# Four transformer layers on one core: the first two weight jobs behind a norm or a merge run as one, row by row

## The chip, the cores and the metric

The kernel runs on one core of one Trainium2 chip. The time is device microseconds (us) for one execution. The profiled execution is a separate one, with its own time.

## The reference, cut to what matters

The input is x, 256 tokens by 1024 features in float32. Two blocks of two layers each are applied one after the other; the kernel calls them A and B.

```python
# block A, each of 2 layers
h = rms_norm(x) @ w_in                      # three kinds of attention, their outputs in mix
x = x + mix @ w_o
gate, up = split(rms_norm(x) @ w_gate_up)   # 2816 + 2816 columns
x = x + (silu(gate) * up) @ w_down
# block B, each of 2 layers
u = rmsnorm(x) @ w_in                       # pooling, convolution, dilated attention, three gates
merged = g0 * br_a + g1 * br_b + g2 * br_c
x = x + rmsnorm(merged @ w_out)
x = x + rmsnorm(memory_cross_attention(rmsnorm(x), mem))
u = rmsnorm(x) @ w_up                       # ua, ub: 2816 + 2816 columns
x = x + rmsnorm((silu(conv(ua)) * ub) @ w_down)
```

## The kernel before, in words

**Layout.** x lies with features on the partitions: 8 row tiles of 128 features by 256 tokens (KD = 8, T = 256). A float32 product is made of three matmuls on rounded halves: high and low part of the weights (`weights_hi`, `weights_lo`) and of x (`x_hi`, `x_lo`), without low times low. One 128x128 weight tile with its three matmuls of 256 columns is the unit of all dense work.

**Jobs and chunks.** The dense work is a list of jobs (`q0`, `gate3`, `out1`, ...). Most make two output tiles of 128 features, so they read 16 weight tiles, first the 8 rows of the first output tile, then those of the second. The weights are packed on the host in the order of use into chunks of at most 12 tiles (128x1536). SyncE loads chunks into 5 raw buffers. ScalarE makes `weights_hi` from a chunk (`split_hi`, L636), VectorE makes `weights_lo` (`split_lo`, L647); chunks 0 and 1 of each layer are done by GpSimd instead (`pool_lo`, L660, chosen by `of_pool`). There are 4 split buffers: chunk c may be split when TensorE has released chunk c-4. `cut()` begins a new chunk early.

**Order.** The lists `order_a` and `order_b` are written by hand, and every engine walks the same list and does its part of each entry, strictly in that order. At each job entry ScalarE and VectorE first split all chunks up to `last_chunk(job) + 2`, and then do the job's own work. `last_chunk(name)` is the chunk of the last row of the last tile, `tiles[-1][-1][1]` (L622). An engine that waits at one entry does nothing of the later ones.

```python
# order_a around gate0, order_b around the merge and out0
("job", "o2"), ("front", ("n2", 1)), ("front", ("n2", 2)), ("job", "gate0"), ("adds", "n2"),
("job", "up0"), ("mean", "n2"), ("job", "gate1"), ("factor", "n2")
("job", "ma3"), ("merge_hi", 2), ("merge_lo", 2), ("job", "mb3"), ("job", "mc3"), ("merge_hi", 3),
("merge_lo", 3), ("job", "out0"), ("mem_split", 0), ("job", "out1"), ("mem_split", 1), ("job", "out2"),
("root_table", "out"), ("job", "out3"), ("job", "mk0a"), ("mem_keys", "mk0a"), ("norm", "p1"), ("spread", "p1")
```

**Behind a norm.** `front` entries write x_hi (ScalarE, L890) and x_lo (VectorE, L900) row tile by row tile, as x becomes known. The factor of the norm is applied later; `squares`, `adds`, `mean` and `factor` find it beside the products: ScalarE squares x (L894), GpSimd adds the pairs (L834, L836), VectorE adds the rest (L855, L858), TensorE sums over the partitions (L908), ScalarE takes the root (L914). In block B the norms p1, p2 and p3 of an output are a serial chain between two jobs: ScalarE squares and scales what out3, mo3 or down3 made (`scalar_y`, L2123 and L2125), adds, TensorE L867, ScalarE L817, VectorE, TensorE L877, then VectorE renews x by row tiles (L2338, L2340). Meanwhile TensorE runs a few `keep_busy` matmuls on zeros (L708).

**The first job** behind a norm or the merge runs in `first_products`: first all products with x_hi (L732, L735), then those with x_lo (L741). Its partner, the second job, runs in the ordinary loop `products` (L775, L777, L778). The pairs are gate0 and up0 in A, q0 and k0, out0 and out1, ua0 and ub0 in B. q0, out0 and ua0 take the high products by row (`ROWS_FIRST`); gate0 takes them tile by tile.

**The merge.** For each of four column pairs i, the jobs ma, mb, mc give the branches; VectorE multiplies each by its gate (L2430) and adds (L2434), ScalarE writes x_hi (L2225), VectorE x_lo (L2357). out0 to out3 follow.

**PSUM.** A job takes the bank used least recently, of 3 banks, or of 6 if its name is in a list; `start_use` waits until the bank's last reader is done.

## Time and profile before

| what | us |
|---|---|
| median of 3 runs | 1700.1 |
| lowest, highest of them | 1691.17, 1700.37 |
| the profiled execution, its own time | 1694.4 |
| its span, first to last instruction | 1692.6 |
| TensorE busy in the span | 1653.9 |
| VectorE, ScalarE, GpSimd busy | 1194.5, 895.7, 114.7 |

A matmul counts as busy until its modelled end, and matmuls overlap, so the pace of TensorE is read from the distance between starts. In a timeline row the first number is the start in us from the span's start, the second how long the row lasts; x4 at the end means four instructions merged.

### The profile page before, as it was taken

To read this page: it belongs to the slowest core of one execution; us is meant where nothing else is said; L and a number is where in the kernel's file an instruction comes from. 1 tells how busy PE (TensorE), PEld (TensorE's weight loads), DVE (VectorE), ACT (ScalarE), POOL (GpSimd) and SP (SyncE) were. 2 spreads that over 40 slices of the span, in tenths; PEclk is the share of its full clock that TensorE was granted. 3 is DMA by queue.
4 is the path that set the end of the run, shared out by engine and by line. 5 is a ranking of instruction groups with operands and counts; after the bars stand their busy time and mean duration, and the time that the engine had idled before them with its cause. 6 is when DMAs were issued, how large, how long until landed. Compare 5 with 4: busy or idle time off the path is not lost.

```text
span 1692.6 us, 31850 instructions
## 1 busy us (share of the span) xinstructions
PE 1653.9 (98%) x13590; PEld 1591.9 (94%) x13590; DVE 1194.5 (71%) x1745; ACT 895.7 (53%) x1366; POOL 114.7 (7%) x72
## 2 busy tenths in 40 slices
PE   9989999999999999999999999999999999999997
PEld 9978999999879999989999989999899999899997
DVE  5887767547976775476858758983667768669963
ACT  5575544454675444544545765554435446655542
POOL 2020000020110000210000110000200001010000
PEclk9999999999999999999999999999999999999999
DMA  8313555553225655555345435654445345345650
GB/s 291 110 58 119 198 188 181 177 189 129 94 76 187 207 198 181 202 185 182 118 149 170 155 109 196 209 182 168 165 167 169 132 160 195 119 138 197 207 188 37
DMA packets 52830, 274.31 MB, mean 162 GB/s; under 512 B 6096, under 2 KB 6736, under 8 KB 52560
## 3 DMA queue, kind: packets, MB, share of 16 engines
q1 hardware_dynamic: 52544, 271.22, 46.9%
q8 instruction: 107, 1.75, 0.4%
q10 hardware_dynamic: 144, 1.05, 0.2%
q14 instruction: 35, 0.29, 0.1%
HBM read 271.19 MB, written 1.05 MB: 161 GB/s over the span
## 4 chain that ended last, share of the span: by engine, by line
PE 77%; DVE 15%; ACT 4%; issue 2%; DMA 1%; POOL 0%; SPq 0%; ACTq 0%; DVEq 0%; POOLq 0%
PE bank L775 16%; PE bank L777 16%; PE bank L778 16%; DVE weights_lo L647 3%; PE scores L775 3%; PE scores L777 3%; PE scores L778 3%; PE heads L775 2%; PE heads L777 2%; PE heads L778 2%; ACT weights_hi L636 1%; PE scores L1849 1%; ACT probs L1170 1%; PE heads L1877 1%; DVE x_lo L900 1%
## 5 line engine op out<-in xcount | busy, mean ns | idle before, releaser
L647 DVE TENSOR_TENSOR weights_lo<-raw,weights_hi 128x1536 fp32r<-128x1536 f32 (+2 forms) x344 | 584.1, 1715 | 232.3 <-ACT weights_hi L636 232.0
L636 ACT ACTIVATE weights_hi<-raw 128x1536 fp32r<-128x1536 f32 (+4 forms) x352 | 499.8, 1440 | 191.1 <-PE bank L778 82.3
L775 PE MATMUL bank<-x_hi,weights_lo 128*128 128x256 f32 (+1 forms) x1600 | 450.1, 281 | 1.0 <-DVE weights_lo L647 1.0
L777 PE MATMUL bank<-x_lo,weights_hi 128*128 128x256 f32 (+1 forms) x1600 | 443.5, 277 | 0.0
L778 PE MATMUL bank<-x_hi,weights_hi 128*128 128x256 f32 (+1 forms) x1600 | 443.4, 277 | 0.0
L775 PEld LDWEIGHTS bank<-x_hi,weights_lo 128*128 128x128 f32 (+1 forms) x1600 | 298.9, 187 | 6.8 <-issue 4.1
L777 PEld LDWEIGHTS bank<-x_lo,weights_hi 128*128 128x128 f32 (+1 forms) x1600 | 300.0, 187 | 2.0 <-issue 2.0
L778 PEld LDWEIGHTS bank<-x_hi,weights_hi 128*128 128x128 f32 (+1 forms) x1600 | 298.7, 187 | 0.0
L775 PE MATMUL bank<-hidden_hi,weights_lo 128*128 128x256 f32 x704 | 196.3, 279 | 0.7 <-DVE hidden_lo L2194 0.7
L777 PE MATMUL bank<-hidden_lo,weights_hi 128*128 128x256 f32 x704 | 196.0, 278 | 0.0
L778 PE MATMUL bank<-hidden_hi,weights_hi 128*128 128x256 f32 x704 | 196.0, 278 | 0.0
L775 PEld LDWEIGHTS bank<-hidden_hi,weights_lo 128*128 128x128 f32 x704 | 132.8, 189 | 1.2 <-DVE hidden_lo L2194 1.1
L777 PEld LDWEIGHTS bank<-hidden_lo,weights_hi 128*128 128x128 f32 x704 | 132.9, 189 | 0.0
L778 PEld LDWEIGHTS bank<-hidden_hi,weights_hi 128*128 128x128 f32 x704 | 132.1, 188 | 0.0
L775 PE MATMUL scores<-x_hi,weights_lo 128*128 128x256 f32 x416 | 115.5, 278 | 0.9 <-DVE weights_lo L647 0.9
L777 PE MATMUL scores<-x_lo,weights_hi 128*128 128x256 f32 x416 | 115.4, 277 | 0.0
L778 PE MATMUL scores<-x_hi,weights_hi 128*128 128x256 f32 x416 | 115.4, 277 | 0.0
L834 POOL TENSOR_TENSOR squares<-squares 128x512 f32<-128x512 f32 x28 | 52.3, 1868 | 829.6 <-ACT squares L2123 638.1
L775 PEld LDWEIGHTS scores<-x_hi,weights_lo 128*128 128x128 f32 x416 | 78.1, 188 | 1.2 <-issue 1.2
L777 PEld LDWEIGHTS scores<-x_lo,weights_hi 128*128 128x128 f32 x416 | 78.5, 189 | 0.0
L778 PEld LDWEIGHTS scores<-x_hi,weights_hi 128*128 128x128 f32 x416 | 78.2, 188 | 0.0
L775 PE MATMUL heads<-x_hi,weights_lo 128*128 128x256 f32 x256 | 71.5, 279 | 0.4 <-DVE weights_lo L647 0.4
(410 smaller groups left out, 3392.3 us busy)
## 6 DMA issues: line engine op xcount, KB each, us to landing
raw<-in_w_b SPq DMA_DIRECT2D x194, 768.0 KB, 4.2
raw<-in_w_a SPq DMA_DIRECT2D x120, 768.0 KB, 4.2
raw<-in_w_a SPq DMA_DIRECT2D x16, 512.0 KB, 3.7
raw<-in_w_b SPq DMA_DIRECT2D x10, 512.0 KB, 3.9
raw<-in_w_b SPq DMA_DIRECT2D x2, 752.0 KB, 4.6
raw<-in_w_a SPq DMA_DIRECT2D x2, 736.0 KB, 7.7
raw<-in_w_b SPq DMA_DIRECT2D x2, 720.0 KB, 4.9
raw<-in_w_a SPq DMA_DIRECT2D x2, 672.0 KB, 6.7
```

The source lines that it names most:

```text
L636: nc.scalar.activation(whi[c % SPLIT][:, 0:n], raw[c % RAW][:, 0:n], ACT.Copy).then_inc(*s.mark("weights_hi", c))
L647: nc.vector.tensor_tensor(wlo[c % SPLIT][:, 0:n], raw[c % RAW][:, 0:n], whi[c % SPLIT][:, 0:n].bitcast(F32), ALU.subtract).then_inc(*s.mar ...
L775: ins = nc.tensor.matmul(dst, wl, xh, start=start, stop=False, skip_group_check=skip)
L777: nc.tensor.matmul(dst, wh, xl, start=False, stop=False, skip_group_check=skip)
L778: ins = nc.tensor.matmul(dst, wh, xh, start=False, stop=stop, skip_group_check=skip)
L834: nc.gpsimd.tensor_tensor(sq[:, 0:2, :], sq[:, 0:2, :], sq[:, 2 * n:2 * n + 2, :], ALU.add).then_inc(*s.mark("sq_pairs", (tag, n)))
L900: nc.vector.scalar_tensor_tensor(out=XL[:, k, :], in0=X[:, k, :], scalar=gains(k), in1=XH[:, k, :].bitcast(F32), op0=ALU.mult, op1=ALU.sub ...
L1170: ins = nc.scalar.activation(PA[c][:, m, :], score_bank[c][:, m * T:(m + 1) * T], ACT.Exp, scale=f[:, m:m + 1], bias=ROW[:, r + m:r + m + ...
L1849: ins = nc.tensor.matmul(dil_scores(h, m, g), QKB[r, f // 2, m * P:(m + 1) * P], QKB[r, 6 + f // 2, 0:dil_tiles(m) * P], start=True, stop= ...
L1877: ins = nc.tensor.matmul(out_bank[rows, m * P:(m + 1) * P], VB[:, kt, f * DHD:(f + 1) * DHD], PTB[:, g * kts + kt, :], start=(n == 0), sto ...
```

## The change: what it does

1. The four pairs of jobs (`PAIRED`) run as one in `first_products`: per row tile k the high products of all four output tiles, row by row, and after all rows the low products in the same order. Both banks are taken at the start. gate0 and up0 go through the rows in the order 6, 7, 0 to 5 (`ROW_ORDER`).
2. Their weights are packed in that order (`Both`): a row has 4 tiles, a chunk 3 rows, so a pair takes chunks of 12, 12 and 8 tiles. With the cuts, gate0/up0 has chunks 26 to 28 of A, q0/k0 0 to 2, out0/out1 43 to 45 and ua0/ub0 59 to 61 of B. Before, gate0 had 26 and 27 with 8 tiles each, up0 28 and 29; both streams keep 72 and 104 chunks. down3 of both blocks begins a chunk.
3. The splits move: at the end of the layer before, chunk 2 of B too (`scalar_next_chunks`, `vector_next_chunks`); `AHEAD` says how far each job splits; out0's chunks with rows 3 to 7 (44, 45) get their low part on GpSimd; gate0 splits up to `last_chunk + 1`, and the front of row tiles 4 and 5 up to `last_chunk("gate0")`. At `squares` only n2 still splits first.
4. `adds` of n3 stands before ua0. down2 in A and p3_sum in B take the second oldest bank; out0 and out1 may use all 6.

```diff
                 stream.cut()
+class Both:
+    def __init__(self, names, stream, source, operand, cols, row_order):
+        self.names = names
+        self.jobs = [Job(name, stream, source, operand, [], []) for name in names]
+        for job, c in zip(self.jobs, cols):
+            job.tiles = [[None] * KD for _ in c]
+        for k in row_order:
+            for job, c in zip(self.jobs, cols):
+                for t, columns in enumerate(c):
+                    job.tiles[t][k] = (k,) + stream.add(source, k * P, P, columns)
+PAIRED = (("gate0", "up0"), ("q0", "k0"), ("out0", "out1"), ("ua0", "ub0"))
+ROW_ORDER = {"gate0": (6, 7, 0, 1, 2, 3, 4, 5)}
+def rows_of(name):
+    return ROW_ORDER.get(name, tuple(range(KD)))
...
+
+    def both(first, second, source, operand, *c):
+        pair = Both((first, second), stream, source, operand, c, rows_of(first))
+        jobs.update(zip(pair.names, pair.jobs))
...
     stream.cut()
-    for i in range(KF // 2):
-        job(f"gate{i}", "w_gate_up", "x2", cols(i * T, 2), full, cut=i == 0)
+    both("gate0", "up0", "w_gate_up", "x2", cols(0, 2), cols(FF, 2))
+    stream.cut()
+    for i in range(1, KF // 2):
+        job(f"gate{i}", "w_gate_up", "x2", cols(i * T, 2), full)
         job(f"up{i}", "w_gate_up", "x2", cols(FF + i * T, 2), full)
     for i in range(4):
         job(f"down{i}", "w_down", "h", cols(i * T, 2), even(KF))
-        if i < 2:
+        if i < 3:
...
     q, k, v, gates = 4 * CW, 4 * CW + AW, 4 * CW + 2 * AW, 4 * CW + 3 * AW
-    for i in range(AW // T):
-        job(f"q{i}", "w_in_2", "x", cols(q + i * T, 2), full, cut=i == 0)
+    both("q0", "k0", "w_in_2", "x", cols(q, 2), cols(k, 2))
+    stream.cut()
+    for i in range(1, AW // T):
+        job(f"q{i}", "w_in_2", "x", cols(q + i * T, 2), full)
...
         job(f"mc{i}", "w_branch_c_2", "dil", cols(i * T, 2), even(2))
-    for i in range(4):
+    stream.cut()
+    both("out0", "out1", "w_out_2", "merged", cols(0, 2), cols(T, 2))
+    for i in range(2, 4):
...
         job(f"mo{i}", "w_mo_2", "memo", cols(i * T, 2), even(MEM_H))
-    for i in range(KF2 // 2):
-        job(f"ua{i}", "w_up_2", "x3", cols(i * T, 2), full, cut=i == 0)
+    stream.cut()
+    both("ua0", "ub0", "w_up_2", "x3", cols(0, 2), cols(FF2, 2))
+    for i in range(1, KF2 // 2):
+        job(f"ua{i}", "w_up_2", "x3", cols(i * T, 2), full)
         job(f"ub{i}", "w_up_2", "x3", cols(FF2 + i * T, 2), full)
     for i in range(4):
+        if i == 3:
+            stream.cut()
...
-            def __init__(self, number, s, stream, jobs, uses, operands, wide_ring):
+            def __init__(self, number, s, stream, jobs, uses, operands, wide_ring, second_oldest=()):
                 self.number, self.s, self.stream, self.jobs = number, s, stream, jobs
                 self.names, self.freed, self.at = [name for name, _ in uses], dict(uses), {}
                 oldest = list(range(BANKS + 3))
                 for name in self.names:
-                    n = next(n for n in oldest if n < BANKS or name.startswith(wide_ring))
+                    n = [n for n in oldest if n < BANKS or name.startswith(wide_ring)][1 if name in second_oldest else 0]
...
                 self.of_pool = set()
-                self.hi_ahead, self.pool_ahead = 0, 0
+                self.hi_ahead, self.lo_ahead, self.pool_ahead = 0, 0, 0
...
                 after.hi_next, after.s.layer, after.s.writing = 0, m, "scalar"
-                split_hi(after, act, m, 1)
+                upto = 1 if after is plan_a else 2
+                split_hi(after, act, m, upto)
                 pl.hi_next, pl.s.layer = here, layer
-                after.hi_ahead = 2
+                after.hi_ahead = upto + 1
+        def vector_next_chunks(pl, dve, l):
+            after, m = next_layer(pl, l)
+            if after is plan_b:
+                here, layer = pl.lo_next, pl.s.layer
+                after.lo_next, after.s.layer, after.s.writing = 2, m, "vector"
+                split_lo(after, dve, m, 2)
+                pl.lo_next, pl.s.layer = here, layer
+                after.lo_ahead = 3
...
         WAITS = {"p1_sum": 3, "p1_factor": 3, "p2_sum": 7, "p2_factor": 3, "ua0": 7, "p3_sum": 7, "p3_factor": 3, "q0": 7}
-        def first_products(pl, pe, l, name, hi_ready):
-            s, job = pl.s, pl.jobs[name]
-            ps = start_use(pl, pe, l, name)
-            keep_busy(ps, WAITS.get(name, 0) if name != "q0" or l else 0)
-            if name == "cq0" and l == 0:
+        def first_products(pl, pe, l, names, hi_ready):
+            s, jobs = pl.s, [pl.jobs[name] for name in names]
+            banks = [start_use(pl, pe, l, name) for name in names]
+            keep_busy(banks[0], WAITS.get(names[0], 0) if names[0] != "q0" or l else 0)
+            if names[0] == "cq0" and l == 0:
                 pe.wait_ge(*O.at(0, "eps"))
-                keep_busy(ps, 44)
-            hi, lo, ready = pl.operands[job.operand]
-            steps = [(t, k) + job.tiles[t][k][1:] for t in range(len(job.tiles)) for k in range(KD)]
-            by_rows = sorted(steps, key=lambda step: step[1]) if name in ROWS_FIRST else steps
+                keep_busy(banks[0], 44)
+            hi, lo, ready = pl.operands[jobs[0].operand]
+            steps = [(j, t, k) + job.tiles[t][k][1:] for j, job in enumerate(jobs) for t in range(len(job.tiles)) for k in range(KD)]
+            by_rows = sorted(steps, key=lambda step: rows_of(names[0]).index(step[2]))
+            paired, last_row = len(jobs) > 1, rows_of(names[0])[-1]
             for low in (False, True):
-                for n, (t, k, c, o, rows, width) in enumerate(steps if low else by_rows):
-                    dst = ps[0:width, t * T:(t + 1) * T]
+                for j, t, k, c, o, rows, width in by_rows if paired or (not low and names[0] in ROWS_FIRST) else steps:
+                    dst = banks[j][0:width, t * T:(t + 1) * T]
+                    whole = low and k == last_row and t == len(jobs[j].tiles) - 1
                     if not low:
                         if c != pl.chunk_at:
                             pe.wait_ge(*s.at(l, *pl.raw_mark(c)))
                             pl.chunk_at = c
-                        if t == 0:
+                        if j + t == 0:
                             pe.wait_ge(*s.at(l, *hi_ready(k)))
-                        ins = nc.tensor.matmul(dst, wlo[c % SPLIT][0:rows, o:o + width], hi[0:rows, k, :], start=(n == 0), stop=False,
+                        first = t == 0 and k == rows_of(names[0])[0]
+                        ins = nc.tensor.matmul(dst, wlo[c % SPLIT][0:rows, o:o + width], hi[0:rows, k, :], start=first, stop=False,
                                                skip_group_check=True)
                         free_split(pl, ins)
                         nc.tensor.matmul(dst, whi[c % SPLIT][0:rows, o:o + width], hi[0:rows, k, :], start=False, stop=False,
                                          skip_group_check=True)
                     else:
-                        if t == 0:
+                        if j + t == 0:
                             pe.wait_ge(*s.at(l, *ready(k)))
-                            pl.ready.add((job.operand, k))
-                        ins = nc.tensor.matmul(dst, whi[c % SPLIT][0:rows, o:o + width], lo[0:rows, k, :], start=False, stop=(k == KD - 1),
+                            pl.ready.add((jobs[0].operand, k))
+                        ins = nc.tensor.matmul(dst, whi[c % SPLIT][0:rows, o:o + width], lo[0:rows, k, :], start=False, stop=(k == last_row),
                                                skip_group_check=True)
-                        if n < len(steps) - 1:
+                        if not whole:
                             free_split(pl, ins)
                         if o + width == pl.stream.used[c]:
                             pl.unfreed = c
-            ins.then_inc(*s.mark("filled", name))
+                        if whole:
+                            ins.then_inc(*s.mark("filled", names[j]))
...
             "mix": (MH, ML, lambda k: ("dif_lo", k // 2) if k < DIF_H else ("mix_lo", k)),
-            "h": (HH, HL, lambda k: ("hidden_lo", k))}, ("gate", "up", "o3", "dq0", "dk0", "g0", "g1", "kv", "flip_dq", "flip_dk0", "flip_g"))
+            "h": (HH, HL, lambda k: ("hidden_lo", k))}, ("gate", "up", "o3", "dq0", "dk0", "g0", "g1", "kv", "flip_dq", "flip_dk0", "flip_g"), ("down2",))
...
                     nc.tensor.matmul(ps[:, 0:2], ones[0:DIF_D, :], ROW[0:DIF_D, 40:42], start=True, stop=True).then_inc(*s.mark("filled", "lam_sum"))
-                elif kind == "job" and name in ("cq0", "gate0"):
-                    first_products(pl, pe, l, name, lambda k: ("norm_hi", ("n1" if name == "cq0" else "n2", k)))
+                elif kind == "job" and name == "cq0":
+                    first_products(pl, pe, l, ("cq0",), lambda k: ("norm_hi", ("n1", k)))
+                elif kind == "job" and name == "gate0":
+                    first_products(pl, pe, l, ("gate0", "up0"), lambda k: ("norm_hi", ("n2", k)))
+                elif kind == "job" and name == "up0":
+                    continue
...
                     scalar_front(pl, act, l, tag, i, lambda k: gain_a(g, k), lambda k: ("x_new", f"{source}{k // 2}"))
+                    if (tag, i) == ("n2", 2):
+                        split_hi(pl, act, l, pl.last_chunk("gate0"))
...
                     if name not in NO_SPLITS:
-                        split_hi(pl, act, l, pl.last_chunk(name) + 2)
+                        split_hi(pl, act, l, pl.last_chunk(name) + (1 if name == "gate0" else 2))
...
                     tag, i = name
+                    if (tag, i) == ("n2", 2):
+                        split_lo(pl, dve, l, pl.last_chunk("gate0"))
...
                     if name not in NO_SPLITS:
-                        split_lo(pl, dve, l, pl.last_chunk(name) + 2)
+                        split_lo(pl, dve, l, pl.last_chunk(name) + (1 if name == "gate0" else 2))
                     ps = pl.bank(name)
                     if name in ("dv0", "dv1"):
                         continue
                     elif name[0] == "o" or name.startswith("down"):
                         i = int(name[-1])
+                        if name == "down3":
+                            vector_next_chunks(pl, dve, l)
...
         order_b += [("front", ("n3", i)) for i in range(4)] + [("squares", "n3"),
-                    ("job", "ua0"), ("adds", "n3"), ("job", "ub0"), ("mean", "n3"), ("job", "ua1"), ("factor", "n3")]
+                    ("adds", "n3"), ("job", "ua0"), ("job", "ub0"), ("mean", "n3"), ("job", "ua1"), ("factor", "n3")]
...
             "merged": (XH, XL, lambda k: ("merged_lo", k // 2)), "memo": (OMH, OML, lambda k: ("memo_lo", k)),
-            "h": (HH2, HL2, lambda k: ("hidden_lo", k))}, ("ua", "ub", "ma", "mb", "mc"))
-        plan_b.of_pool = {0, 1}
+            "h": (HH2, HL2, lambda k: ("hidden_lo", k))}, ("ua", "ub", "ma", "mb", "mc", "out0", "out1"), ("p3_sum",))
+        merge_chunks = {jobs_b["out0"].tiles[0][k][1] for k in range(3, KD)}
+        plan_b.of_pool = {0, 1} | merge_chunks
+        AHEAD = {"mc3": 3, "out0": 1, "out2": 3, "out3": 3, "mo2": 3, "mo3": 3, "q0": 1, "ua0": 1}
...
                 elif kind == "job" and name in first_of_b:
-                    first_products(pl, pe, l, name, first_of_b[name])
+                    names = next((pair for pair in PAIRED if pair[0] == name), (name,))
+                    first_products(pl, pe, l, names, first_of_b[name])
+                elif kind == "job" and name in ("k0", "out1", "ub0"):
+                    continue
...
                 elif kind == "squares":
-                    split_hi(pl, act, l, pl.last_chunk({"n1": "q0", "n2": "mq0", "n3": "ua0"}[name]) + 2)
+                    if name == "n2":
+                        split_hi(pl, act, l, pl.last_chunk("mq0") + 2)
...
                     if name not in own_splits:
-                        split_hi(pl, act, l, pl.last_chunk(name) + (3 if name in ("out1", "out2", "out3") else 2))
+                        split_hi(pl, act, l, pl.last_chunk(name) + AHEAD.get(name, 2))
...
             pl, s = plan_b, B
-            pl.lo_next = 0
+            pl.lo_next, pl.lo_ahead = pl.lo_ahead, 0
...
                     if name not in own_splits:
-                        split_lo(pl, dve, l, pl.last_chunk(name) + (3 if name in ("out1", "out2", "out3") else 2))
+                        split_lo(pl, dve, l, pl.last_chunk(name) + AHEAD.get(name, 2))
+                    if name == "down3":
+                        vector_next_chunks(pl, dve, l)
...
                 elif kind == "job":
-                    pool_lo(pl, pool, l, pl.last_chunk(name) + 2)
+                    pool_lo(pl, pool, l, pl.last_chunk(name) + (3 if name == "mc3" else 2))
```

## Rows read from the trace of the kernel before

**Rows 1.** Who waited for whom, TensorE: us in total, times, longest

```profile
PE scores L732 <- ACT x_hi L890: 2.5, 6, 0.6
```

**Rows 2.** Timeline of TensorE, first and last of 39 matmuls on end

```profile
799.75 0.28 PE L775 MATMUL bank<-x_hi,weights_lo 128*128 128x256 f32 x1
...
804.06 0.28 PE L778 MATMUL bank<-x_hi,weights_hi 128*128 128x256 f32 x1
```

**Rows 3.** Timeline of TensorE in A, layer 0: first of gate0, first of gate1

```profile
173.65 0.28 PE L732 MATMUL scores<-x_hi,weights_lo 128*128 128x256 f32 x1
...
187.10 0.36 PE L775 MATMUL bank<-x_hi,weights_lo 128*128 128x256 f32 x1
```

**Rows 4.** Timelines of VectorE, GpSimd and ScalarE beside gate0 and up0

```profile
174.97 4.23 DVE L900 SCALAR_TENSOR_TENSOR x_lo<-x,gains_a,x_hi 128x256 fp32r<-128x256 f32 x4
...
179.12 3.41 DVE L647 TENSOR_TENSOR weights_lo<-raw,weights_hi 128x1536 fp32r<-128x1536 f32 x2
...
178.11 0.81 POOL L836 TENSOR_TENSOR squares<-squares 128x256 f32<-128x256 f32 x1
...
187.28 0.26 ACT L914 ACTIVATE norm_root<-turned,row 128x4 f32<-128x4 f32 x1 [4.33 <-PE turned L908]
```

**Rows 5.** GpSimd's split L660: count and durations in ns, min/median/max

```profile
L660 POOL TENSOR_TENSOR weights_lo<-raw,weights_hi x8: 2351/2400/2612, 9.7 to 1183.6; 128x1024 fp32r<-128x1024 f32 x8
```

**Rows 6.** Timelines from the merge to p1 in B, layer 0, by engine

```profile
914.19 0.63 ACT L2225 ACTIVATE x_hi<-t 128x512 fp32r<-128x512 f32 x1 [4.04 <-DVE t L2434]
...
916.60 0.39 PE L732 MATMUL bank<-x_hi,weights_lo 128*128 128x256 f32 x1 [0.25 <-DVE t L2430]
...
923.75 0.60 ACT L2123 ACTIVATE squares<-bank 128x512 f32<-128x512 f32 x1 [0.41 <-PE bank L741]
...
924.96 1.71 ACT L1981 ACTIVATE mem_hi<-mem,gains_b 128x256 fp32r<-128x256 f32 x4
...
928.99 0.28 PE L775 MATMUL bank<-x_hi,weights_lo 128*128 128x256 f32 x1
...
935.98 1.28 ACT L812 ACT_TABLE_LOAD   x1
...
937.38 2.88 ACT L636 ACTIVATE weights_hi<-raw 128x1536 fp32r<-128x1536 f32 x2
...
940.17 0.58 ACT L2123 ACTIVATE squares<-bank 128x512 f32<-128x512 f32 x1
...
942.68 0.42 DVE L858 TENSOR_TENSOR squares<-squares 128x256 f32<-128x256 f32 x1
```

**Rows 7.** Timelines of ScalarE and TensorE at the passage from A to B

```profile
701.22 1.28 ACT L2650 ACT_TABLE_LOAD   x1
...
704.66 2.49 ACT L890 ACTIVATE x_hi<-x,gains_b 128x256 fp32r<-128x256 f32 x6
...
706.52 0.36 PE L732 MATMUL bank<-x_hi,weights_lo 128*128 128x256 f32 x1 [0.82 <-DVE x L1673]
```

**Rows 8.** Timelines of ScalarE, TensorE and VectorE at ua0, B, layer 0

```profile
994.00 1.07 ACT L636 ACTIVATE weights_hi<-raw 128x1024 fp32r<-128x1024 f32 x1
...
1003.50 0.36 PE L732 MATMUL scores<-x_hi,weights_lo 128*128 128x256 f32 x1
...
1007.49 3.25 DVE L900 SCALAR_TENSOR_TENSOR x_lo<-x,gains_b,x_hi 128x256 fp32r<-128x256 f32 x8
...
1018.46 0.36 PE L775 MATMUL heads<-x_hi,weights_lo 128*128 128x256 f32 x1
```

**Rows 9.** Timelines of GpSimd and TensorE at q0, B, layer 1

```profile
1188.74 0.73 POOL L836 TENSOR_TENSOR squares<-squares 128x256 f32<-128x256 f32 x1
...
1194.32 0.36 PE L732 MATMUL bank<-x_hi,weights_lo 128*128 128x256 f32 x1
...
1209.61 0.36 PE L775 MATMUL bank<-x_hi,weights_lo 128*128 128x256 f32 x1
```

**Rows 10.** Busy time by engine, granted clock, DMA share and GB/s, one stretch

```profile
143.50:150.00 6.50, 4.72 (x27) 4.75 (x28) 5.61 (x9) 2.30 (x9) 0.00 (x0) 0.74 0.49 147
```

3 lines of the change are left out of this document (added).

## The prediction

> **What bounds the kernel now.** I read the page first: TensorE is busy for 1653.9 of 1692.6 us, so only the places where it waits, and what the edits put in its way, can move the time. The waits of TensorE come next: the largest entry that the change aims at is the wait of the high products for x_hi, 2.5 us in six pieces [rows 1]. Short waits fall under that view's threshold, so I took the pace from the timeline: 38 steps from 799.75 to 804.06, 0.1134 us a matmul [rows 2]. A pair of jobs is 96 matmuls, 10.9 us at this pace. Whatever lies between the first matmul of a pair and the first of the next job beyond 10.9, and 0.4 for the four small `mean` matmuls, is lost. gate0 and up0 take 13.45 [rows 3]: 2.2 lost. ua0 and ub0 take 14.96 [rows 8]: 3.7 lost. q0 and k0 of B's second layer take 15.29 [rows 9]: 4.0. out0 and out1 take 12.39 and start 0.4 late [rows 6]: 1.9. q0 of B's first layer, and cq0 of A's second, wait 0.8 each for a bank [rows 7]. With both layers that is 4.4 + 7.4 + 4.0 + 3.8 + 1.6 = 21 us, 1.25%: the most that the change can win.
>
> **The change part by part.** Two prices first. ScalarE: two high splits of 1536 columns run from 937.38 to 940.17, so 1.4 each [rows 6]; 1024 columns take 1.1 [rows 8]. VectorE: two low splits take 3.41, so 1.7 each [rows 4]; two thirds of it for 1024, 1.2.
>
> *ua0 and ub0.* The first high product starts when row 0 of x_hi is there, at 1003.50. Rows then come about every 0.65 us: VectorE has renewed x when it turns to x_lo at 1007.5 [rows 8], and the last x_hi follows 1.0 later. A row now feeds 8 matmuls, 0.91 us, so TensorE waits 0.3 in all, ends the high products at 1011.05 and the low ones at 1014.7; with the mean ua1 starts at 1015.1 and not 1018.46 [rows 8]: 3.4 won. Against it: chunks 60 and 61 are both split at mo2. ScalarE had one of 1024 at 994.00 [rows 8]; now 1.4 + 1.1, so the squares of mo2 come 0.75 later, and VectorE has 1.7 + 1.2 of low splits where GpSimd adds squares. They block each other (below), and the sum of p2 is 1.3 late, on the serial chain. Net 2.1 won, 4.2 in two layers; bounds 2 and 7.
>
> *out0 and out1, low parts on GpSimd.* GpSimd took 2.40 us for 1024 columns [rows 5]; in proportion 3.6 for 1536, less some fixed part 3.5. ScalarE splits chunk 44 at job mb3, and `merge_hi 2` stands before that: x_hi of the third pair starts at 914.19 [rows 6], so chunk 44's high part is ready at 916.2 and chunk 45's at 917.7. GpSimd is through with 44 at 920.4 and with 45 at 924.6. TensorE starts at 916.2 (the bank wait is gone, 0.4 won), wants chunk 44 for row 3 at 918.9 and chunk 45 at 923.3: it waits 1.6 and 1.3. The low products end at 930.15; out2 started at 928.99 before [rows 6], so 1.2 is lost here.
>
> How GpSimd and VectorE hinder each other is in the timeline: eight x_lo take 3.25 us alone [rows 8], four take 4.23 while GpSimd adds squares [rows 4]. [...]
>
> *out0 and out1, the work behind them.* This is the larger part. Both jobs now end together at 930.0, and ScalarE walks its list: y of out0 1.2 (from 923.75 to 924.96), four mem_hi 1.6, chunk 47, y of out1, four mem_hi, chunks 48 and 49, y of out2, the root table 1.4 (935.98 to 937.38), chunks 50 and 51, and only then the squares of out3 [rows 6]. Before, out0's y and chunk 47 were done by 928. Sum: 3 x 1.2 + 2 x 1.6 + 5 x 1.4 + 1.4 = 15.2, so the squares start at 945.3, not 940.17 [rows 6]. VectorE's low part of chunk 51 and the adds behind it end at 948.1, not 943.1 [rows 6]. Nothing covers it: TensorE has mk0a, and then the serial chain of p1. It is 5.0 later with the 1.2 of before in it; 10.0 in two layers. Bounds 3 (if ScalarE catches up) and 12.
>
> *gate0 and up0.* The x_hi rows cost nothing any more: rows 6 and 7 were there first, a row lasts 0.91. But the order of rows meets `last_chunk`: it takes the chunk of row 7, and by `ROW_ORDER` row 7 is in the first of three chunks, 26, not 28. So the new split at the front asks for 26 and does nothing, gate0 asks for 27, up0 for 28. Chunk 28 comes after `adds`, which waits for GpSimd (its last add ends at 178.92, [rows 4], now 0.5 later since chunk 27 has 1536 columns) and for the x_lo that it held up: ready at 182.2. TensorE wants it for row 4 at 173.65 + 48 x 0.1134 = 179.1. It waits 3.2; rows 4 and 5 to 184.1, the low products to 187.75, the mean to 188.2. Before, up0 asked for chunk 31; now chunk 29 is asked for at gate1, and on ScalarE `mean` stands before gate1: L914 waits for TensorE's mean (187.28 after 187.1 before, [rows 4]). So root 0.2, high split 1.4, low split 1.7: chunk 29 is ready at 191.7. gate1 starts at 191.8, not 187.10 [rows 3]: 4.7 lost, 9.4 in two layers. Bounds: 2.2 won a layer if both splits were in time, 5.5 lost.
>
> *q0 and k0, first layer of B.* ScalarE now waits for chunk 2's buffer until 2.7 us (8 tiles) before down3's end, 0.8 and some before 706.52, so 702.8, then 1.1, to 703.9. Behind it stand the sine tables and the root table, 3.45 from 701.22 to 704.66, which ended just in time [rows 7]. x_hi starts at 707.35 and TensorE at 708.0, not 706.52 [rows 7]: 1.5 later, of which 0.1 comes back. 1.4 lost; bounds -0.8 and 2.5. cq0 in A's second layer loses the 0.8 wait and waits 0.1 for x_hi: 0.7 won.
>
> *q0 and k0, second layer of B.* The rows bring 3.1 as at ua0. But GpSimd has chunks 0 and 1 with 1536 columns: 3.5 each and not 2.4 [rows 5], and VectorE chunk 2 at the same moment. GpSimd's last add for p3 ended at 1189.47 [rows 9], 0.8 before it was wanted; now all of them end at 1191 to 1192.5, and the chain of p3 is 1.9 late. The rest of the win goes into the mean, whose sum is ready at 1209.2. q1 starts at 1209.7 against 1209.61 [rows 9]: 0, bounds -3 and 2.
>
> *The rest.* 16 tiles more or less in a chunk and the other cuts change no totals: the same tiles, 72 and 104 chunks, DMAs of the same bytes. down2's and p3_sum's banks have been free for 15 us.
>
> **Sum.** 9.4 + 10.0 + 1.4 - 0.7 + 0 - 4.2 = +15.9 us on the profiled execution's 1694.4: 1710.3. That execution was 5.7 under the median; the four times shown have the mean 1696.5, which gives 1712.4. I say 1712, 0.7% over the median. About 1%, 17 us, is what a measurement of this kernel tells from no change, since its own runs lie 9 us apart.
>
> **The rivals.** *The rows win.* All splits hide, and 15 to 21 us of the lost time go: 1676 to 1682. It needs chunks 28 and 29 early, against the code's own order, and ScalarE free behind out1. Chance 0.04. *One of the two large costs is absent* (chunk 29 in time, or the squares of out3 in time): 1700 to 1704. For it speaks that ScalarE is busy only 53% of the span; against it that it works its list in order. 0.26. *Forecast*: 1706 to 1717, 0.45. *The clock falls, and the time ends slower:* TensorE would idle 3.3 to 4 us at four new places, chunks 28 and 29 in both layers of A and before p1's sum in B. [...] Four to six such stretches add 7 to 10: 1719 to 1722. 0.25, with other late waits of the same kind in it.
>
> **How the numbers follow.** Slower by over 1% (over 1717) has the last rival and a part of the forecast's upper end: 0.36. Faster by over 1% (under 1683) is the first: 0.03. The rest, 0.61, is within 1%. The range goes from 1696, under the half-cost case, to 1723, the clock's.
>
> **What would show it.** In the profile after: TensorE waiting for weights_lo (L647) before row 4 in gate0 and again at gate1, 3 us each, in both layers, with ScalarE's root directly before chunk 29; L660 with 12 entries, four of them in the merges, 3.5 us long; the squares of out3 5 us later after the merge; ua1 2 us earlier. If gate1 starts within 12 us of gate0, my reading of `last_chunk` is wrong, and the time is near 1703; if the squares of out3 follow out3 at once, the same. If both, the kernel is faster than before.

## The result, and the profile after

The changed kernel takes 1725.97 us (median of 4: 1718.01 to 1728.56), the kernel before 1698.69 beside it (median of 4: 1691.17 to 1700.37). The ratio is 1.0163, 95% interval 1.0139 to 1.0188: 1.6% slower. The profiled execution took 1724.51, its span is 1722.7, 30.1 more than before. (The medians differ by 27.3: the profiled execution of before lay 4.3 under its median.) From the page of the changed kernel, busy time, share and instructions:

```profile
PE 1659.4 (96%) x13590; PEld 1600.9 (93%) x13590; DVE 1205.8 (70%) x1741; ACT 894.3 (52%) x1366; POOL 135.6 (8%) x76
```

TensorE's busy time rose by 5.5 us only (1653.9 before), so most of the 30 is idle time. GpSimd has 20.9 us more (114.7 before), its larger and added splits.

**Waits.** TensorE's waits in the changed kernel (us in total, times, longest), against [rows 1]:

```profile
PE bank L834 <- DVE weights_lo L691: 11.5, 6, 3.6
PE bank L926 <- DVE squares L917: 10.8, 5, 2.8
PE scores L790 <- POOL weights_lo L704: 4.8, 4, 1.5
PE scores L790 <- DVE weights_lo L691: 4.6, 2, 2.5
PE bank L790 <- ACT x_hi L949: 2.4, 1, 2.4
PE bank L834 <- DVE gates L2486: 1.2, 2, 0.6
```

The six waits of the high products for x_hi [rows 1] are gone; the one of 2.4 is another, new one, at q0 of B's first layer. In their place TensorE waits for low parts of weights: from VectorE in gate0 (4.6) and at gate1 (3.6 in each layer, 7.2 of the 11.5), from GpSimd in out0 (4.8), and for the squares ahead of a norm's sum (L926; 2.65 at p1 of B's first layer).

**gate0, up0 and gate1** in A's first layer, timelines of ScalarE, VectorE and TensorE, against [rows 3, 4]:

```profile
178.33 1.05 ACT L680 ACTIVATE weights_hi<-raw 128x1024 fp32r<-128x1024 f32 x1
189.18 0.26 ACT L973 ACTIVATE norm_root<-turned,row 128x4 f32<-128x4 f32 x1 [9.81 <-PE turned L967]
189.34 2.84 ACT L680 ACTIVATE weights_hi<-raw 128x1536 fp32r<-128x1536 f32 x2
...
176.88 4.22 DVE L959 SCALAR_TENSOR_TENSOR x_lo<-x,gains_a,x_hi 128x256 fp32r<-128x256 f32 x4
181.02 0.41 DVE L914 TENSOR_TENSOR squares<-squares 128x256 f32<-128x256 f32 x1
181.81 1.22 DVE L691 TENSOR_TENSOR weights_lo<-raw,weights_hi 128x1024 fp32r<-128x1024 f32 x1
190.85 1.76 DVE L691 TENSOR_TENSOR weights_lo<-raw,weights_hi 128x1536 fp32r<-128x1536 f32 x1 [1.19 <-ACT weights_hi L680]
...
183.08 0.39 PE L790 MATMUL scores<-x_hi,weights_lo 128*128 128x256 f32 x1 [2.46 <-DVE weights_lo L691]
192.75 0.55 PE L834 MATMUL bank<-x_hi,weights_lo 128*128 128x256 f32 x1 [3.61 <-DVE weights_lo L691]
```

gate0 starts at 175.02. Chunk 28 is the one of 1024 columns: its high part is done at 179.38, its low part stands behind four x_lo and the adds (181.81) and ends at 183.03; TensorE goes on at 183.08. Chunk 29's high part stands behind the root of the norm (189.18), its low part ends at 192.61, and gate1 starts at 192.75: 17.73 behind gate0, not 13.45 [rows 3]. The second layer has 17.60 against 13.11.

**The clock.** Three stretches: start and end, length, busy time and number of instructions by engine (TensorE first), granted clock, DMA share and GB/s:

```profile
186.00:189.00 3.00, 3.00 (x29) 3.00 (x27) 0.00 (x0) 0.00 (x0) 0.00 (x0) 1.00 0.12 51
192.00:198.50 6.50, 5.75 (x27) 5.78 (x28) 5.61 (x4) 4.21 (x4) 0.00 (x0) 0.50 0.75 238
724.50:727.50 3.00, 3.00 (x16) 3.00 (x15) 2.34 (x6) 3.00 (x8) 0.09 (x1) 0.50 1.00 392
```

Behind the 3.6 us wait at gate1 the granted clock is 0.50, matmuls start 213 ns apart instead of 113, and the stretch loses 2.8 us; the second layer 1.6 (0.50 from 544.0 to 546.5), and q0 of B, behind its 2.4 us wait, 1.6. With fillers in the wait at gate1 (run 2 below) the clock behind it is 1.00, and 4.2 us of this come back.

**out0, out1 and the work behind them** in B's first layer, timelines of GpSimd, VectorE, ScalarE and TensorE, against [rows 5, 6]:

```profile
935.94 7.83 POOL L704 TENSOR_TENSOR weights_lo<-raw,weights_hi 128x1536 fp32r<-128x1536 f32 x2 [177.96 <-ACT weights_hi L680]
...
935.84 0.69 DVE L2511 TENSOR_TENSOR t<-t,merge_part 128x512 f32<-128x512 f32 x1
936.57 0.69 DVE L2507 SCALAR_TENSOR_TENSOR merge_part<-gates,bank 128x512 f32<-128x512 f32 x1
937.29 3.13 DVE L2511 TENSOR_TENSOR t<-t,merge_part 128x512 f32<-128x512 f32 x1
941.19 3.13 DVE L2432 SCALAR_TENSOR_TENSOR x_lo<-t,x_hi 128x512 fp32r<-128x512 f32 x1 [0.77 <-ACT x_hi L2300]
...
949.54 0.60 ACT L2197 ACTIVATE squares<-scores 128x512 f32<-128x512 f32 x1 [7.08 <-PE scores L799]
964.77 0.58 ACT L2197 ACTIVATE squares<-bank 128x512 f32<-128x512 f32 x1
...
939.92 0.39 PE L790 MATMUL scores<-x_hi,weights_lo 128*128 128x256 f32 x1 [1.51 <-POOL weights_lo L704]
943.82 0.38 PE L790 MATMUL scores<-x_hi,weights_lo 128*128 128x256 f32 x1 [0.90 <-POOL weights_lo L704]
967.80 0.61 PE L926 MATMUL bank<-const,squares 128*128 128x2 f32 x4 [2.65 <-DVE squares L917]
```

GpSimd's two splits take 3.9 each, and TensorE waits 1.51 and 0.90 for them. ScalarE stands idle for 7.1 us and then has the work of both jobs at once: the squares of out3 begin at 964.77, 29.2 behind out0's start (935.53); before it was 23.6 [rows 6]. Two instructions of VectorE that take 0.69 take 3.13 beside GpSimd's splits; both have two inputs in SBUF. L2507, with an input from PSUM, took 0.69 in between. The slow two end at 940.42 and 944.32, each 0.55 behind the end of the split that was running (939.86 and 943.77).

### The profile page after: what moved, and what is told of

Its sections match the earlier page's. It is cut to its first block, busy times and chain, and to the rows that moved or that the text cites. A ratio compares the mean times of both kernels' runs of the same rounds, so it can differ in the third digit from the quotient of the medians.

```text
span 1722.7 us, 31845 instructions
## 1 busy us (share of the span) xinstructions
PE 1659.4 (96%) x13590; PEld 1600.9 (93%) x13590; DVE 1205.8 (70%) x1741; ACT 894.3 (52%) x1366; POOL 135.6 (8%) x76
## 4 chain that ended last, share of the span: by engine, by line
PE 75%; DVE 13%; ACT 6%; issue 3%; POOL 2%; DMA 0%; SPq 0%; ACTq 0%; DVEq 0%; POOLq 0%
PE bank L834 15%; PE bank L837 14%; PE bank L836 14%; PE scores L834 3%; PE scores L837 3%; PE scores L836 3%; DVE weights_lo L691 3%; ACT weights_hi L680 3%; PE heads L837 1%; PE heads L836 1%; PE heads L834 1%; POOL weights_lo L704 1%; DVE x_lo L959 1%; ACT probs L1229 1%; PE heads L1948 1%
## 5 line engine op out<-in xcount | busy, mean ns | idle before, releaser
L834 PE MATMUL bank<-x_hi,weights_lo 128*128 128x256 f32 (+1 forms) x1536 | 436.3, 284 | 9.9 <-DVE weights_lo L691 8.7
L836 PE MATMUL bank<-x_lo,weights_hi 128*128 128x256 f32 (+1 forms) x1536 | 429.2, 279 | 0.0
L837 PE MATMUL bank<-x_hi,weights_hi 128*128 128x256 f32 (+1 forms) x1536 | 429.2, 279 | 0.0
L834 PEld LDWEIGHTS bank<-x_hi,weights_lo 128*128 128x128 f32 (+1 forms) x1536 | 289.0, 188 | 16.2 <-issue 12.8
L836 PEld LDWEIGHTS bank<-x_lo,weights_hi 128*128 128x128 f32 (+1 forms) x1536 | 291.3, 190 | 2.0 <-issue 2.0
L837 PEld LDWEIGHTS bank<-x_hi,weights_hi 128*128 128x128 f32 (+1 forms) x1536 | 288.7, 188 | 0.0
L704 POOL TENSOR_TENSOR weights_lo<-raw,weights_hi 128x1536 fp32r<-128x1536 f32 (+1 forms) x12 | 39.3, 3287 | 922.6 <-ACT weights_hi L680 922.6
```

What stands on the lines that cost most here:

```text
L704: nc.gpsimd.tensor_tensor(wlo[c % SPLIT][:, 0:n], raw[c % RAW][:, 0:n], whi[c % SPLIT][:, 0:n].bitcast(F32), ALU.subtract).then_inc(*s.mar ...
L834: ins = nc.tensor.matmul(dst, wl, xh, start=start, stop=False, skip_group_check=skip)
L836: nc.tensor.matmul(dst, wh, xl, start=False, stop=False, skip_group_check=skip)
L837: ins = nc.tensor.matmul(dst, wh, xh, start=False, stop=stop, skip_group_check=skip)
```

## The experiments

Each kernel is the changed one with the edit shown. Ratios are to the kernel before, in the same rounds. "out0 to mk0b" is the distance of the first matmuls of these jobs.

**1. last_chunk mended.**

```diff
-                return self.jobs[name].tiles[-1][-1][1]
+                return max(step[1] for tile in self.jobs[name].tiles for step in tile)
```

> The changed kernel with one line changed: last_chunk returns the highest chunk number of a job, not that of its row 7. gate0 and up0 then have 28 as their last chunk, so chunks 26 to 28 are split ahead of the third front, 29 at gate0 and 30 at up0. My theory: the late chunks 28 and 29 are the whole loss of gate0/up0 and of the clock spell behind them. TensorE's waits of 2.1 to 3.6 us before row 4 and before gate1 go, so does the half-speed stretch after gate1: 2 x 4.4 + 2.8 + 1.6 = 13 us less than the changed kernel, near 1713; if the row order then also brings its own gain of up to 2 a layer, 1709. Rival 1: chunks 27 and 28 now stand in front of x_lo and the squares on VectorE and ScalarE, 5 us of VectorE's work, so the low products wait instead: only 2 to 6 us less, 1720 to 1724. Rival 2: the loss comes from somewhere else: no difference.

Measured: 1708.96, ratio 1.0082 (1.0053 to 1.0111), the lower of the two times that the theory gave. gate0 to gate1 takes 11.24 and 11.67, gate1 to gate2 11.64 in both layers (14.45 and 13.23 in the changed kernel). Timeline of VectorE:

```profile
176.65 1.92 DVE L959 SCALAR_TENSOR_TENSOR x_lo<-x,gains_a,x_hi 128x256 fp32r<-128x256 f32 x2
178.66 1.22 DVE L691 TENSOR_TENSOR weights_lo<-raw,weights_hi 128x1024 fp32r<-128x1024 f32 x1
179.80 2.40 DVE L959 SCALAR_TENSOR_TENSOR x_lo<-x,gains_a,x_hi 128x256 fp32r<-128x256 f32 x2
182.12 1.75 DVE L691 TENSOR_TENSOR weights_lo<-raw,weights_hi 128x1536 fp32r<-128x1536 f32 x1
```

Chunk 28's low part now stands between the x_lo and ends at 179.9, not 183.0, and 29's ends at 183.9. x_lo is late for nobody. By the ratios this one accident cost about 14 us of the 27; at its own places in the two traces 16.8 are gone (12.4 up to gate1, 4.4 behind it).

**2. Fillers in the waits:** matmuls on zeros whose results nobody reads, so that TensorE isn't idle there.

```diff
+            if pl.number == 0 and name == "gate1":
+                keep_busy(ps, 12)
...
-            keep_busy(banks[0], WAITS.get(names[0], 0) if names[0] != "q0" or l else 0)
+            keep_busy(banks[0], WAITS.get(names[0], 0))
```

> The changed kernel, with matmuls on zeros in two waits: 12 (0.27 us each, 3.3 us) between up0 and gate1, where TensorE waits 3.6 us for chunk 29, and 7 (1.9 us) in the 2.4 us before q0 of B's first layer. All waits stay, only TensorE isn't idle in them. If what follows the waits is lost to the clock (half of full speed for 6.8 us after gate1 in A's first layer, shorter in the second and after B's q0), those stretches run at full clock and the kernel is 2.8 + 1.6 + 1.6 = 6 us faster than the changed one, near 1720. If the slow stretches have another cause, there is no difference, or it is slower by what the fillers are too long, at most 1 us.

Measured: 1718.58, ratio 1.0132 (1.0100 to 1.0164). Fillers and first matmul of gate1 on TensorE's timeline:

```profile
189.73 2.92 PE L763 MATMUL bank<-quiet 128*128 128x128 f32 x24
193.38 0.39 PE L836 MATMUL bank<-x_hi,weights_lo 128*128 128x256 f32 x1 [0.73 <-DVE weights_lo L691]
```

The clock of the stretch behind them, and of one behind the wait in gate0, which had no fillers:

```profile
193.50:199.00 5.50, 5.50 (x47) 1.00 0.84 255
182.50:185.00 2.50, 2.50 (x13) 0.50 0.73 216
```

gate1 to gate2 fell to 11.85 and 11.66: 2.6 and 1.6 regained with the same wait in front. Of the 15 kernels traced, the six whose gate1 waits 3.6 without fillers have 13.1 to 14.5 there in all twelve layers (granted clock 0.50 from 0.2 to 1.7 us behind the wait), the eight without the wait (the kernel before among them) 11.6 in all sixteen (1.00). So the loss there is the clock's, caused by the idle time. At q0 of B the run settles nothing: q0 to q1 took 11.33, but also in the next kernel, which had no fillers there. The half-speed stretch inside gate0 at 182.5, 1.5 us, came in 6 of the 14 layers that have the wait of 2.1 to 2.5 us there (granted clock 0.50 to 0.52 from 0.2 to 1.7 us behind it, 1.00 in the other eight), and not in the changed kernel's own trace.

**3. The memory's splits early.**

```diff
-        order_b += [("job", "out0"), ("mem_split", 0), ("job", "out1"), ("mem_split", 1), ("job", "out2"), ...
+        order_b += [("mem_split", 0), ("mem_split", 1), ("job", "out0"), ("job", "out1"), ("job", "out2"), ...
```

> The changed kernel with the splits of the memory's rows (mem_split 0 and 1, 8 x 0.52 us on ScalarE, 8 x 0.48 on VectorE) ahead of out0 in the written order, not behind out0 and out1. My theory, that ScalarE is late at p1 because it can only start its list when out0 and out1 end together: 4.2 us of that list then lie in the wait, mk0b starts up to 3 us earlier in each layer, 5 to 6 us less in all, near 1720. Rival, that the late p1 is due to GpSimd's splits or to TensorE itself: no difference, or slower, since VectorE's mem_lo now stand in front of the low split of chunk 46.

Measured: 1719.23, ratio 1.0138 (1.0094 to 1.0181). out2 to mk0a fell from 11.9 to 10.9, mk0a to mk0b from 8.0 to 5.8, in both layers: 3.2 each, as the theory has it, of the 5.7 and 5.5 that out0 to mk0b had lost. ScalarE's list behind the pair is the larger part of this pair's loss.

**4. Only two chunks ahead between A and B.**

```diff
-                upto = 1 if after is plan_a else 2
+                upto = 2 if pl is plan_b and after is plan_b else 1
...
-            if after is plan_b:
+            if pl is plan_b and after is plan_b:
...
+                    if name == "n1" and l == 0:
+                        split_hi(pl, act, l, 2)
```

> The changed kernel, but between A and B only chunks 0 and 1 are split ahead, and chunk 2 of B's first layer behind the fronts, as before; between B's two layers all three stay ahead. My theory: the 2.4 us that TensorE waits for x_hi before q0 come from ScalarE's wait for chunk 2's buffer, in front of the sine tables. Then the wait falls below 1 us and with it the slow clock after it: 1.6 + 1.6 = 3.2 us less than the changed kernel, near 1723; chunk 2 is wanted 5.4 us into the pair and comes in time, or up to 1 us late, which would leave 2 us. Rival: x_hi is late for another reason (the pairing alone): no difference.

Measured: 1717.32, ratio 1.0125 (1.0096 to 1.0154). down3 to q0 takes 15.5 instead of 18.1, and q0 to q1 11.75 instead of 12.97: 3.8 us. Chunk 2 comes in time.

**5. out0 and out1 apart,** low parts on VectorE.

```diff
-    both("out0", "out1", "w_out_2", "merged", cols(0, 2), cols(T, 2))
-    for i in range(2, 4):
+    for i in range(4):
...
-        plan_b.of_pool = {0, 1} | merge_chunks
-        AHEAD = {"mc3": 3, "out0": 1, "out2": 3,
+        plan_b.of_pool = {0, 1}
+        AHEAD = {"out1": 3, "out2": 3,
```

> The changed kernel with out0 and out1 as two jobs again, their low parts on VectorE and the splits asked for as before; the other three pairs stay. My theory: this pair cost what the traces show between the starts of out0 and mk0b, 5.3 a layer (GpSimd's splits 1.6, ScalarE's late list 1.0 and 3.0, less 0.4 at the start): 10.6 us less than the changed kernel, and the wait for the squares before p1's sum (2.7 us) is gone. Rival: the wait before p1 has another cause, such as VectorE's adds or the two more chunks that mo2 asks for: at most 5 us less.

Measured: 1719.83, ratio 1.0157 (1.0123 to 1.0192), a miss. Two of TensorE's waits in it:

```profile
PE bank L789 <- ACT x_hi L2298: 5.1, 2, 2.6
PE bank L762 <- DVE y L2411: 5.1, 1, 5.1
```

mk0a to mk0b was back at 4.93 and out2 to mk0a at 10.88, as before the change [rows 6], so p1 is mended. But without the pair the banks fall differently: q0 and k0 of B's second layer now want the bank of p3_factor and wait 5.1 for its last reader. And out0 waits 2.6 for the last x_hi of the merge, so that out0 to out2 stays at 13.95 and 15.61 (12.39 before the change).

**6. The pair's low parts on VectorE.**

```diff
-        plan_b.of_pool = {0, 1} | merge_chunks
+        plan_b.of_pool = {0, 1}
```

> The changed kernel with the low parts of chunks 44 and 45 on VectorE (1.7 us each) instead of GpSimd (3.5 us each); the pair stays. My theory: the waits of 1.5 and 0.9 us inside the pair go, so out2 starts 1.6 earlier, and the rest of the loss (ScalarE's list, 4.0 a layer) stays: 3.3 us less than the changed kernel in two layers. [...] Rival, that VectorE is short of time in the merge: x_lo and the gate products come later, no gain or 1 to 2 us more.

Measured: 1726.58, ratio 1.0187 (1.0167 to 1.0207). out0 to out2 fell to 12.89, 1.0 to 1.2 a layer; everything behind stayed. A half-speed stretch around mk0b (granted clock 0.50 from 966.5 to 969.4, 1.4 us) took it back in the first layer, and the run as a whole is no faster than the changed kernel; the 3.3 us of the theory aren't seen. The waits of 1.51 and 0.90 are gone, but the pair now waits for the last x_hi of the merge, 1.8 at the longest, since VectorE has the splits to do as well. GpSimd is not what makes p1 late.

**7. Three repairs, all pairs kept** (1, 3 and 4 together).

> The changed kernel with three repairs at once, all four pairs kept: last_chunk by the highest chunk, the memory's splits ahead of out0, two chunks ahead between A and B. Each took off in its own trace, place by place: 16.8 (gate0/up0 with the clock), 6.3 (out), 3.8 (start of B). My theory that these losses lie at separate places and add up: 27 us less than the changed kernel's profiled execution, or 21 to 24 less than its median: 1697 to 1704, 0 to 0.6% above the kernel before. Rival, that they overlap (a wait mended at one place comes back behind): 1706 or more.

Measured: 1697.66, ratio 1.0021 (1.0001 to 1.0042). The losses do add up, and with them gone the four pairs together still win nothing. ScalarE's timeline in the merge shows the idle time used:

```profile
922.34 0.64 ACT L2302 ACTIVATE x_hi<-t 128x512 fp32r<-128x512 f32 x1 [3.20 <-DVE t L2513]
922.88 3.29 ACT L2052 ACTIVATE mem_hi<-mem,gains_b 128x256 fp32r<-128x256 f32 x8
926.07 1.48 ACT L680 ACTIVATE weights_hi<-raw 128x1536 fp32r<-128x1536 f32 x1
931.24 0.60 ACT L2197 ACTIVATE squares<-scores 128x512 f32<-128x512 f32 x1 [3.70 <-PE scores L799]
```

**8. Out apart, mended, ua0's splits as before:** edits 1, 4 and 5, and on ScalarE and VectorE

```diff
-        AHEAD = {... "mo2": 3, "mo3": 3, "q0": 1, "ua0": 1}
+        AHEAD = {... "q0": 1, "ua0": 1}
...
+                    if name == "n3":
+                        split_hi(pl, act, l, pl.last_chunk("ua0"))
```

> The changed kernel with out0/out1 as two jobs, last_chunk by the highest chunk, two chunks ahead between A and B, and the splits for ua0 asked for as before (chunk 60 at mo3, chunk 61 behind the fronts). Theory: the three pairs that wait for a norm then win what the rows allow against the kernel before: gate0/up0 2.2 and 1.4 as measured with last_chunk mended, ua0/ub0 3.0 and 3.5 with the delay of 1.4 each at p2 gone, cq0 0.5, q0/k0 of B's second layer 0.8: 11 to 12 us less than before, near 1684. Rival: the splits put back behind the fronts are late again for row 6 (as chunk 28 was in the changed kernel), and the win stays at 6 to 8: 1687 to 1690. Rival: pairing wins nothing beyond the scatter: within 0.3% of before.

Measured: 1704.77, ratio 1.0066 (1.0039 to 1.0093), above the theory and both rivals. The late split of the first rival is there:

```profile
1513.23 0.58 PE L789 MATMUL scores<-x_hi,weights_lo 128*128 128x256 f32 x1 [3.04 <-DVE weights_lo L690]
```

mo0 to ua0 was back at 16.8 (18.2 in the changed kernel), so the early splits do cost 1.4 at p2 (1.3 in the forecast). But ua0 to ua1 took 15.1 and 17.6 instead of 11.6 to 11.9. In the second layer half speed follows the wait (granted clock 0.50):

```profile
1513.30:1519.00 5.70, 5.70 (x27) 0.50 0.46 143
```

The early split is cheaper, by 1.8 and 4.5 a layer. Not all of the distance to the theory is the late split's: this run has both accidents of run 5 again, 5.1 for the bank and 5.1 for the x_hi of the merge.

**9. Out apart again:** edit 5, and

```diff
     for i in range(4):
         job(f"ma{i}", ...), job(f"mb{i}", ...), job(f"mc{i}", ...)
-    stream.cut()
...
-        ... ("ua", "ub", "ma", "mb", "mc"), ("p3_sum",))
+        ... ("ua", "ub", "ma", "mb", "mc"))
```

> The changed kernel with out0 and out1 as two jobs, as in the earlier run of this kind, but with two things of the kernel before put back that this run had left: no cut ahead of out0 (with the cut the third pair's x_hi stood behind a split that waited for its buffer, TensorE waited 2.5 us for it), and p3's banks in the plain order (with the other one q0 and k0 waited 5.1 us for the bank of p3_factor). Theory: out0 to mk0b then takes 28.2 us a layer as before the change, 5.3 less than in the changed kernel; with the two accidents gone the kernel is 10 us under the changed one, 1714 to 1717. Rival: the pair's loss isn't what the traces show, and it stays at 1720 or above.

Measured: 1720.5, ratio 1.0155 (1.0131 to 1.0178), the rival's number, but not for the rival's reason. The bank's wait is gone; the wait for x_hi isn't, it is 3.3 us. My reason for it was wrong: it isn't the cut, but the q0/k0 layout, which moves all chunk boundaries of B up to the merge by 4 tiles, and so one more low split of 1.76 ahead of the last sums of the merge on VectorE; with the old layout, in run 12, out0 to out2 is back at 12.39 and 12.68.

**10. Three pairs** (9 with 1 and 4), and **11.** the same with chunk 2 behind the fronts in both layers of B.

> The same, with last_chunk by the highest chunk and only two chunks ahead between A and B: the three pairs that stand behind a norm, without the accidents. Theory: against the kernel before it wins 1.8 and 1.4 at gate0/up0 (11.67 instead of 13.45 and 13.11), 2.1 a layer at ua0/ub0, 0.8 at q0/k0 of B's second layer, 0.5 at cq0, 0.5 at the start of B, and loses 1 to 2 in places that the new cut moves (B's gates, hidden_lo): 7 to 8 us under before, ratio 0.995 to 0.996. Rival 1: a half-speed stretch of 1.6 to 3 us in front of q0 or ua0 eats a part: 0.997 to 0.999. Rival 2: the pairs win nothing: 1.000.

> The kernel with three pairs, but chunk 2 of B's second layer too is split behind the fronts, not ahead in the first layer's down3. Theory: the path from down1 to q0 (p3's sum, root, factor and fronts), 1.8 us longer in the changed kernel than before, has one source in the low split of chunk 2 on VectorE (1.2 us) and the wait of ScalarE for its buffer, and one in GpSimd's two splits of 3.5 us: it gets 0.7 to 1.2 shorter, q1 starts 1 us earlier. Rival: GpSimd's splits alone make the 1.8: no difference at this place. Rival: chunk 2 then comes late for row 6, as chunk 61 did for ua0 (3.0 us): 2 to 3 us slower there.

Measured: 1695.45, ratio 1.0003 (0.9987 to 1.0020), and 1698.51, ratio 1.0015 (0.9994 to 1.0035). Neither can be told from before; the 0.995 to 0.996 of the theory is missed. out0 to out2 takes 16.0 in all four layers against 12.39 before: 7.2 us a run lost through the moved boundaries. Of the 3.6 a layer 2.1 are the wait (3.2 for x_hi, 1.1 in run 12), the rest is half speed behind it, as in run 10:

```profile
918.10:921.50 3.40, 3.27 (x15) 0.50 0.07 24
```

In run 11 down1 to q0 was 0.75 shorter and q0 to q1 1.5 longer: the theory's part came, and the late chunk of the second rival took it back and more.

**12. Two pairs:** gate0/up0 (with edit 1) and ua0/ub0; q0, k0, out0, out1 and B's chunks up to the merge as before the change (with the edits of 9 for out0 and out1). **13.** The same with the out0/out1 pair as in the changed kernel.

```diff
-PAIRED = (("gate0", "up0"), ("q0", "k0"), ("out0", "out1"), ("ua0", "ub0"))
+PAIRED = (("gate0", "up0"), ("ua0", "ub0"))                       # run 12
+PAIRED = (("gate0", "up0"), ("out0", "out1"), ("ua0", "ub0"))     # run 13
...
-    both("q0", "k0", "w_in_2", "x", cols(q, 2), cols(k, 2))
-    stream.cut()
-    for i in range(1, AW // T):
-        job(f"q{i}", "w_in_2", "x", cols(q + i * T, 2), full)
+    for i in range(AW // T):
+        job(f"q{i}", "w_in_2", "x", cols(q + i * T, 2), full, cut=i == 0)
```

> Only two pairs: gate0/up0 with last_chunk by the highest chunk, and ua0/ub0. q0, k0, out0, out1 are jobs of their own, B's chunks up to the merge lie as before the change, two chunks are split ahead at every start. Theory: 1.8 and 1.4 won at gate0/up0, 2.1 a layer at ua0/ub0 (3.0 and 3.6 in the pair, less 1.4 at p2's sum) and 0.5 a layer behind it, 1 at the start of A's second layer, 0.7 a layer lost at down0; out0 to mk0b as before (28.2): 7 to 9 us under before, ratio 0.995. Rival 1: a half-speed stretch before ua0 takes 1.3 to 1.6 back in some layers: 0.996 to 0.997. Rival 2: the row order wins nothing that can be measured: 1.000.

> The same with the out0/out1 pair of the changed kernel as well, on the same chunks. Theory: this pair costs 5.3 a layer between the starts of out0 and mk0b, whatever stands before it: 33.5 to 33.9 instead of 28.2 there, 10.6 us more than the two pairs alone, ratio higher by 0.006. Rival, that half of it came from the shifted chunks of the merge in the changed kernel: 5 us more, 0.003.

Measured: 1692.78, ratio 0.9987 (0.9965 to 1.0009), and 1706.3, ratio 1.0072 (1.0049 to 1.0094). In run 12 out0 to mk0b takes 28.20 and 29.02, in run 13 36.43 and 33.56. The second layer shows the 4.5 to 5.3 of the waits, the first 3 us more, with two half-speed stretches that run 12 has not (its clock is 1.00 from 905 to 950; granted clock in run 13):

```profile
924.00:927.00 3.00, 3.00 (x16) 0.51 0.44 180
949.00:954.80 5.80, 5.80 (x28) 0.50 0.47 170
```

Between the medians the out pair costs 13.5 us, above the 10.6 expected: the waits and the clock together. A second, smaller part is an accident of run 13's own, the bank wait of run 5 (5.0 us before q0, of which q0 to q1 gives 3.8 back).

In its own rows run 12 wins most of what was expected: gate0 to gate1 2.2 and 1.4; mo0 to ua3, with the pair in it, 2.1 and 1.5 (2.6 expected). It loses 1.0 and 0.7 at down0. The rest lies in the scatter (1682.71 to 1701.42), so a gain of the pairs themselves, 2.5 us between the medians, isn't shown; the 7 to 9 us of the theory is missed.

## Why the prediction was wrong

The direction, the places and the mechanisms were those forecast; the time, 1725.97, is 3 us above the range's end. The ledger of the span, in both layers together:

| place | forecast | measured |
|---|---|---|
| gate0 to gate1 | +9.4 | +8.8 |
| out0 (start and pair) to mk0b | +10.0 | +10.4 |
| q0, first layer of B | +1.4 | +1.6 |
| cq0, second layer of A | -0.7 | -0.5 |
| q0/k0, second layer of B | 0 | -0.8 |
| mo0 to ua1 | -4.2 | -3.8 |
| sum of the forecast's terms | +15.9 | +15.7 |
| clock at gate1 (2.8, 1.6) and q0 (1.6) | 0 (a rival) | +6.0 |
| B's gates (0.76 a layer), down0 (0.7 a layer) | 0 | +2.9 |
| pace of TensorE in long stretches | 0 | +5.7 |
| rest | 0 | -0.2 |
| span | +15.9 | +30.1 |

**The terms held.** `last_chunk` did what the forecast read in it: chunk 28 was ready 8.0 behind gate0's start (forecast 8.55), gate1 started 17.7 behind it (18.15), and run 1 took both away. The squares of out3 started 29.2 behind out0 (29.1 in the forecast, 945.3 less 916.2; 23.6 before), and run 3 shows the cause, ScalarE's list behind two jobs that end together. Within the out term one part was over-sized: the forecast gave GpSimd's splits waits of 1.6 and 1.3, the changed kernel has 1.51 and 0.90, and by run 6 only 1.0 to 1.2 a layer come back without them, although each split took 3.9 and not 3.5. The 1.4 at p2 that the forecast put at 1.3 is shown by run 8.

**The step that failed is the one from the sum to the time.** The forecast put two waits of over 3 us in each layer of A into the sum and left the clock out of it, as a rival with a chance of 0.25. But these aren't separate cases: where gate1 waited 3.6 us without fillers, the clock fell to 0.50 in every layer of every kernel. This cost 6.0 in three stretches (2.8, 1.6 and 1.6); the rival had 7 to 10 in four to six, an estimate of 1.7 each from the one stretch of before with a mean clock of 0.74 over 6.5 us [rows 10]. Two of the rival's places, chunk 28 and p1's sum, kept the full clock in this execution (1.00 from 183.2 to 186 and from 967 to 972), and q0 of B, which it didn't name, lost it. With 6.0 more the sum would have been near 1718, still 8 short. The chunks of other sizes ("change no totals") were costed at nothing and cost 2.9. Half of that, the 0.76 a layer at B's gates, comes from the moved boundaries: it is there in every run with the q0/k0 layout and gone in runs 12 and 13. The 0.7 a layer at down0, where TensorE waits up to 1.1 for `hidden_lo` and not 0.4, stays in every run; that it too comes from the packing is argued, not shown. The last 5.7 was in no case, and its cause stays open: nothing shows it to be the change's (below), and it is partly the draw of one execution of each kernel.

**Of the rivals,** "one of the two large costs is absent" is excluded by runs 1 and 13, which each show one. "The rows win" named its conditions rightly, last_chunk mended and ScalarE free behind out1, but not its size: run 12 has both and stands at 0.9987, run 7 with all four pairs and its repairs at 1.0021, nowhere near the 15 to 21 us. "The clock falls" was right in kind, and is the missing part of the sum.

## What to carry to other kernels

When products are put in another order, follow every helper that reads "the last" of something from a position; here one such line cost about 14 us, more than the pairs won at all their places together (3.6 at gate0/up0 with the line mended, 3.8 at ua0/ub0, 0.8 at q0/k0, 0.5 at cq0). Two jobs run as one release their results together: put independent work of the engine that reads them ahead of the pair, or its whole list comes late. Here a new wait of 3.6 us on TensorE cost 1.5 to 2.8 us again in the clock behind it, each of twelve times, and one of 2.1 to 2.5 us in gate0 6 times of 14. So put that into the sum, and look what a new packing does to the boundaries far from the edit.
